# Forming the rows of each expert by TensorE products from rows on chip, in place of scatters, row loads and transposes

## What is computed

```python
def moe_swiglu(h, router, wg, wu, wd):
    probs = jax.nn.softmax((h @ router).astype(F32), axis=-1)
    vals, idx = lax.top_k(probs, TOP_K)
    vals = vals / jnp.sum(vals, axis=-1, keepdims=True)
    combine = jnp.sum(jax.nn.one_hot(idx, N_EXPERTS, dtype=F32) * vals[..., None], axis=-2)
    out = jnp.zeros(h.shape, F32)
    for e in range(N_EXPERTS):
        out = out + combine[..., e:e + 1] * swiglu(h, wg[e], wu[e], wd[e]).astype(F32)
    return out.astype(h.dtype)
```

## Time and profile before

| | |
|---|---|
| median of 3 runs | 1541.55 us (1540.8 to 1542.12) |
| profiled execution, its own time | 1543.34 us |
| its span (first to last instruction) | 1541.5 us |
| mean granted TensorE clock | 0.996 |
| TensorE busy | 1511.2 us |
| VectorE, ScalarE, GpSimd busy | 643.9, 404.6, 86.6 us |
| HBM read, written | 473.48 MB, 40.34 MB |
| first expert product | 682.63 us into the span |

### The profile page before, as it was taken

The page is one execution under the profiler, slowest core; times in us unless marked ns, Lnnn a source line. Parts: engine busy times, 40 slices in busy tenths (PEclk is TensorE's granted clock), DMA queues, the critical chain, the costliest instruction groups (busy, mean ns, idle before and its releaser), DMA issues.

```text
span 1541.5 us, 31601 instructions
## 1 busy us (share of the span) xinstructions
PE 1511.2 (98%) x14136; PEld 903.7 (59%) x14136; DVE 643.9 (42%) x1025; ACT 404.6 (26%) x613; POOL 86.6 (6%) x118
## 2 busy tenths in 40 slices
PE   9999999999999999999999999999999999999986
PEld 7888889999999999864333333333333333333322
DVE  7566878677656897551301301301311312112034
ACT  4444666544455547530000010010010000000001
POOL 1122221000000011010000000000000000000001
PEclk9999999999999999999999999999999999999998
DMA  9687786688656545569999999999999999999995
GB/s 373 223 287 268 258 291 216 201 275 280 223 179 209 199 164 196 233 234 418 426 408 427 426 425 427 424 419 429 405 424 430 395 423 427 401 427 416 423 427 249
DMA packets 136937, 515.88 MB, mean 335 GB/s; under 512 B 6488, under 2 KB 58912, under 8 KB 128480
## 3 DMA queue, kind: packets, MB, share of 16 engines
q1 hardware_dynamic: 116672, 450.03, 73.7%
q0 software_dynamic: 15968, 57.97, 10.2%
q10 hardware_dynamic: 4160, 5.84, 1.1%
HBM read 473.48 MB, written 40.34 MB: 333 GB/s over the span
## 4 chain that ended last, share of the span: by engine, by line
issue 53%; PE 37%; DVE 3%; ACT 1%; DMA 1%; POOL 0%; POOLq 0%; ACTq 0%; DVEq 0%
PE ps L2020 35%; DMA ring<-y_scr,expert_arena 1%; PE ps L2233 1%; DVE ring L1458 0%; POOL y_scr L962 0%; ACT ring_low_parts L1019 0%; DVE expert_arena L1969 0%; PE ps L2360 0%; DVE expert_arena L1986 0%; DVE ring_low_parts L1408 0%; DVE expert_arena L1976 0%; DVE expert_arena L1894 0%; ACT arena L1196 0%; PE ps L2481 0%; DVE arena L1748 0%
## 5 line engine op out<-in xcount | busy, mean ns | idle before, releaser
L2020 PE MATMUL ps<-ring,expert_x_turned 128*32 128x448 f32 x5152 | 488.8, 539 | 1.6 <-issue 0.8
L2020 PEld LDWEIGHTS ps<-ring,expert_x_turned 128*32 128x32 f32 x5152 | 169.5, 110 | 318.1 <-issue 316.2
L2020 PE MATMUL ps<-normed_high,ring_low_parts 128*128 128x264 f32 x1344 | 267.2, 290 | 0.4 <-DVE normed_low L1392 0.4
L2020 PE MATMUL ps<-ring,expert_hidden_turned 128*32 128x512 f32 x2360 | 257.4, 595 | 6.0 <-DMA ring<-in_moe_w_down 6.0
L1408 DVE TENSOR_TENSOR ring_low_parts<-ring,ring_low_parts 128x1024 fp32r<-128x1024 f32 (+3 forms) x184 | 209.1, 1142 | 84.6 <-ACT ring_low_parts L1019 84.2
L1019 ACT CAST ring_low_parts<-ring 128x1024 fp32r<-128x1024 f32 (+3 forms) x184 | 180.8, 983 | 222.9 <-PE ps L2020 214.3
L1947 DVE TENSOR_TENSOR expert_arena<-expert_arena,ps 128x1344 f32<-128x1344 f32 (+1 forms) x16 | 23.9, 1496 | 481.8 <-PE ps L2020 481.8
L2020 PEld LDWEIGHTS ps<-normed_high,ring_low_parts 128*128 128x128 f32 x1344 | 214.9, 189 | 5.4 <-issue 4.2
L2020 PEld LDWEIGHTS ps<-ring,expert_hidden_turned 128*32 128x32 f32 x2360 | 76.8, 110 | 184.0 <-issue 174.4
L2020 PE MATMUL ps<-normed_low,ring_low_parts 128*128 128x264 f32 x640 | 159.3, 284 | 0.0
L2020 PE MATMUL ps<-h_parts,ring_low_parts 128*128 128x264 f32 x1056 | 129.6, 285 | 0.0
(11 more groups left out here) (294 smaller groups left out, 1157.0 us busy)
## 6 DMA issues: line engine op xcount, KB each, us to landing
ring<-in_moe_w_gate SPq DMA_DIRECT2D x64, 1792.0 KB, 12.0
ring<-in_moe_w_down SPq DMA_DIRECT2D x47, 2048.0 KB, 13.6
ring<-in_moe_w_up SPq DMA_DIRECT2D x48, 1792.0 KB, 12.2
expert_piece_slot<-in_moe_w_up SPq DMA_DIRECT2D x16, 1792.0 KB, 13.0
ring<-in_ret_w_in SPq DMA_DIRECT2D x8, 2048.0 KB, 11.1
ring<-in_state_retention POOLq DMA_DIRECT2D x32, 512.0 KB, 6.6
out_ret_s<-ring POOLq DMA_DIRECT2D x32, 512.0 KB, 4.0
ring<-in_hg_w_in SPq DMA_DIRECT2D x8, 2048.0 KB, 8.0
```

What stands on the lines that cost most here:

```text
L2020: return nc.tensor.matmul(out, lhsT, rhs, start=first, stop=last)
```

## The change

For every visit the rows are now formed turned, by TensorE from x_tok: `gather_x` takes x_tok itself (every eighth column, 128 of them) as weights and the selection gsel (token by place) as the moving side, so that the sum in PSUM is already xe but for the gain; VectorE multiplies with the gain (`take_expert_x`). That is 8 k x 3 token tiles = 24 products of 128 columns of weights by 96 (64) columns. In the loop they stand behind piece 17 (GATHER_BEHIND) and write banks 6 and 7; VectorE makes the selection of the next visit behind the first hidden transpose. h_tok, the scatters, the row loads, the transposes of xe and the gain rows by partition are gone; the ranks for all experts are kept and swapped by visit (`by_visit`). TensorE also forms rows behind the last visit (for a further round, which here does not come). FEW keeps the places as they are: only visit 7 has 64. The core of the diff:

```diff
-C_LAST = 64
-GROUPS = [TG] * (NE - 1) + [C_LAST // 32]
+C_FEW = 64
+FEW = (7, )
+GROUPS = [C_FEW // 32 if v in FEW else TG for v in range(NE)]
...
-        X_AT, X_AT_LAST = 12, 2
+        GATHER_BEHIND = 17
...
-            def load_rows(i):
-                sp.dma_start(x_row, y_scr[bass.ds(i * C, P), :]).then_inc(x_row_in, 16)
-
             for t in range(EP):
-                if t == X_AT:
-                    sp.wait_ge(x_scattered, 96)
-                    load_rows(2)
...
-                    if t == (X_AT if v < NE - 1 else X_AT_LAST):
-                        sp.wait_ge(xe_ok, i + 1)
-                        load_rows(i + 2)
...
-            freed(pool, ("lv", 4, 3))
-            pool.dma_start(g_row, ins["norm_ffn_g"][1].partition_broadcast(P)).then_inc(rows_in, 16)
-            filled(pool, ("hvar", 0))
-            for c in range(4):
-                pool.dma_start(g_group[32 * c:32 * c + 32, 0, :],
-                               ins["norm_ffn_g"][1][256 * c:256 * c + 256].partition_broadcast(32)).then_inc(rows_in, 16)
-            filled(pool, ("ho", 3))
-            nc.gpsimd.memset(x_tok[:, 2, :], 0.0).then_inc(x_pad_ok, 1)
-            pool.wait_ge(h_tok_ok, 3)
+            pool.dma_start(moe_gain, ins["norm_ffn_g"][1].rearrange("(p k) -> p k", k=KD)).then_inc(rows_in, 16)
             pool.wait_ge(rows_ok, 1)
-            pool.wait_ge(xe_ok, 1)
-            for t in range(3):
-                m = P if t < 2 else NS
-                for w in range(2):
-                    pool.indirect_dma_start(y_scr[:, :], bass.IndirectOffsetOnAxis(ap=rowi[0:m, w, t:t + 1], axis=0),
-                                            h_tok[0:m, t, :], None).then_inc(x_scattered, 16)
...
-            link(V.scalar_tensor_tensor(out=reff, in0=rk[:, 0:3, 0], scalar=1.0, in1=mm_[:, :, 0], op0=ALU.add, op1=ALU.mult))
-            for t in range(3):
-                m = P if t < 2 else NS
-                i = V.tensor_scalar(gsel[0:m, t, :], cc("slot")[0:m], reff[0:m, t:t + 1], rstd_tok[0:m, t:t + 1],
-                                    ALU.is_equal, ALU.mult)
-            i.then_inc(sel_ok, 1)
-            V.tensor_tensor(r1, rk[:, 0:3, :].unsqueeze(1).to_broadcast([P, 2, 3, 8]), oab, ALU.mult)
+            link(V.scalar_tensor_tensor(out=rank_at, in0=rk[:, 0:3, :], scalar=1.0, in1=mm_, op0=ALU.add, op1=ALU.mult))
...
+            def selection(v, numbers):
+
+                for t in range(3):
+                    m = P if t < 2 else NS
+                    i = V.tensor_scalar(gsel[0:m, t, 0:32 * GROUPS[v]], numbers[0:m, 0:32 * GROUPS[v]],
+                                        rank_at[0:m, t, v:v + 1], rstd_tok[0:m, t:t + 1], ALU.is_equal, ALU.mult)
+                i.then_inc(sel_ok, 1)
+
+            def rank_of_further_round(v):
+
+                V.tensor_scalar(rank_at[:, :, v], rank_at[:, :, v], -32.0 * GROUPS[v], None, ALU.add)
+
+            selection(0, cc("slot"))
...
+            link(V.max(fewest, fewest_in))
+            link(V.tensor_scalar(rounds_f[:, 4:5], fewest[:, len(FEW) - 1:len(FEW)], -float(C_FEW), 1.0, ALU.is_lt, ALU.add))
...
+                V.tensor_copy(expert_at, cc("exp8"))
+                V.tensor_copy(places, cc("slot"))
+                link(V.max_index(fewest_ix, fewest, fewest_in))
+                link(V.tensor_copy(fewest_expert, fewest_ix))
+                for n, v in enumerate(FEW):
+                    link(V.tensor_scalar(swap_at, expert_at, fewest_expert[:, n:n + 1], None, ALU.is_equal))
+                    at = swap_at.unsqueeze(1).to_broadcast([P, 10, 8])
+                    link(V.tensor_tensor(swap_tmp, by_visit, at, ALU.mult))
+                    link(V.reduce_sum(swap_of, swap_tmp, AX.X))
+                    link(V.tensor_tensor(swap_by, by_visit[:, :, v], swap_of, ALU.subtract))
+                    link(V.tensor_tensor(swap_tmp, at, swap_by.unsqueeze(2).to_broadcast([P, 10, 8]), ALU.mult))
+                    link(V.tensor_tensor(by_visit, by_visit, swap_tmp, ALU.add))
+                    link(V.tensor_copy(by_visit[:, :, v], swap_of))
+                V.tensor_copy(visit_expert, expert_at).then_inc(order_ok, 1)
...
+                V.tensor_tensor(row_g, rowf, vt, ALU.add)
+                link(V.tensor_tensor(rowi, rowf, vt, ALU.add))
+                dve.sem_inc(rows_ok, 1)
...
-            def normed_rows(t):
-
-                m = P if t < 2 else NS
-                freed(dve, ("tok", t, 1))
-                V.scalar_tensor_tensor(out=h_tok[0:m, t, :], in0=x_tok[0:m, t, :], scalar=rstd_tok[0:m, t:t + 1],
-                                       in1=g_row[0:m, :], op0=ALU.mult, op1=ALU.mult).then_inc(h_tok_ok, 1)
...
+            def take_expert_x(v, q, o):
+
+                w = 32 * GROUPS[v]
+                return V.tensor_tensor(xe[:, 4 * q:4 * q + 4, 0:w], o[:, 0:4 * w].rearrange("p (k s) -> p k s", k=4),
+                                       moe_gain[:, 4 * q:4 * q + 4].unsqueeze(2).to_broadcast([P, 4, w]), ALU.mult)
+
+            dve.wait_ge(rows_in, 32)
+            for q in range(2):
+                filled(dve, ("first", q))
+                i = take_expert_x(0, q, bank(("first", q)))
+                frees(i, ("first", q))
+            freed(dve, ("first", 1))
+            dve.sem_inc(xe_ok, 1)
...
-                t0, t1 = 2 * q, min(2 * q + 2, TG)
-                filled(dve, ("first", q))
-                frees(V.tensor_tensor(first_rows[:, t0:t1], bank(("first", q))[:, 0:256 * (t1 - t0)].rearrange("p (t n) -> p t n", n=256),
-                                      g_group.to_broadcast([P, t1 - t0, 256]), ALU.mult), ("first", q))
-                freed(dve, ("first", q))
-                i = turn_rows(first_rows, t0, t1)
-            i.then_inc(xe_ok, 1)
...
-                    dve.wait_ge(x_row_in, i * 16 + 16)
-                    for t in range(GROUPS[(e + 1) % NE]):
-                        for c in range(4):
-                            j = V.transpose(xe[32 * c:32 * c + 32, :, 32 * t:32 * t + 32],
-                                            x_row[32 * t:32 * t + 32, 256 * c:256 * c + 256].rearrange("p (f b) -> p b f", b=KD))
-                    j.then_inc(xe_ok, 1)
+                        if h == 0:
+                            selection((e + 1) % NE, places)
+                            dve.wait_ge(sel_ok, i + 2)
+                            rank_of_further_round((e + 1) % NE)
...
+                    for q in range(2):
+                        dve.wait_ge(x_full, i * 2 + (q + 1))
+                        j = take_expert_x((e + 1) % NE, q, ps[:, 6 + q, :])
+                    j.then_inc(xe_ok, 1)
...
-            for t in range(TG):
-                q = t // 2
-                if t % 2 == 0:
-                    claim(("first", q))
-                for s in range(3):
-                    freed(pe, ("tok", s, 1))
-                    for c in range(4):
-                        j = mm(bank(("first", q))[32 * c:32 * c + 32, 256 * (t % 2):256 * (t % 2) + 256],
-                               gsel[:, s, 32 * t:32 * t + 32], x_tok[:, s, 256 * c:256 * c + 256], s == 0, s == 2)
-                if t in (1, 2):
-                    close(j, ("first", q))
+            def gather_x(q, o, w):
+
+                for k in range(4 * q, 4 * q + 4):
+                    for s in range(3):
+                        m = P if s < 2 else NS
+                        i = mm(o[:, w * (k % 4):w * (k % 4) + w],
+                               x_tok[0:m, s, :].rearrange("t (p k) -> t k p", k=KD)[:, k, :], gsel[0:m, s, 0:w],
+                               s == 0, s == 2)
+                return i
+
+            for s in range(3):
+                freed(pe, ("tok", s, 1))
+            for q in range(2):
+                claim(("first", q))
+                close(gather_x(q, bank(("first", q)), C), ("first", q))
             freed(pe, ("rk", 0))
             pe.sem_inc(w_used, 1)
-            keep_busy(("hw", 5), 512, 384)
+            keep_busy(("hw", 5), 128)
...
+                        if t == GATHER_BEHIND:
+                            if e == 0:
+                                pe.wait_ge(last_sel_ok, r * TL + (1 + TL))
+                            pe.wait_ge(sel_ok, n + 2)
+                            for q in range(2):
+                                gather_x(q, ps[:, 6 + q, :], 32 * GROUPS[(e + 1) % NE]).then_inc(x_full, 1)
...
+            mm(ps[0:32, last_bank[2], 0:1], ident[:, 0:32], ident[:, 0:1])
+            pe.wait_ge(xe_ok, last + 2)
```

More of the change, by code:

```diff
@@ L491, in hybrid_step @@
         marks = part(earena, RB + 418, 32)
-        last_sel = part(sel_mem, 0, TG, NT)
+        last_sel = part(sel_mem, 0, TL, NT)
         pos_wide = part(earena, 8512, 3, P)
@@ L501, in hybrid_step @@
         ixf = part(earena, RB + 160, 3, 8)
-        oab = part(earena, RB + 184, 2, 3, 8)
+        by_visit = part(tables, 0, 10, 8)
+        expert_at, rank_at = by_visit[:, 0], by_visit[:, 1:4]
+        oab = part(tables, 32, 2, 3, 8)
+        swap_tmp = part(tables, 80, 10, 8)
```

(39 more changed lines are left out.)

52 lines of the change are left out of this document (18 added, 34 removed).

## The result

The changed kernel takes 1685.93 us (median of 4 runs, 1684.88 to 1686.38) against 1541.17 (4 runs, 1539.97 to 1542.12) for the one before: a ratio of 1.0939, interval 1.092 to 1.0958. The forecast was 1595.0 us in a range of 1574 to 1647. The direction was right; the loss of 145 us is almost three times the 53.5 forecast, and lies outside the range. The profiled execution has a span of 1683.8 us at a mean clock of 0.956.

What follows compares the result with a forecast made beforehand. TensorE was taken to bind visits 0 to 6, late weights adding 11.1 us to the last. With g = 7.8 us a gather, 9g - 16.7 gave + 53.5 on 1541.55: 1595.0 us, range 1574 to 1647.

Steps and rivals of the forecast that it cites:

- What bounds the kernel: Expert stage: TensorE has no idle time in visits 0 to 6 (108.21 us each); DMA costs the last visit 11.1 us.
- I take the unit-stride value, since that ratio is VectorE's, and may be the transpose's own price: Gather's weight loads of every eighth float: priced as unit stride, 7.8 us a visit, not doubled to 13.3.
- rival 1: Gather: strided weight loads at half rate, 0.115 us more a record, g 13.3 us, + 103.0, 1644.6 us; chance 0.27.
- g: TensorE's added time for one visit's gather of 48 records: 8 x 0.955 + 0.15 = 7.8 us.
- No clock below 1.0 before it ends: Changed profile's last visit: TensorE's clock not below 1.0 before its end, the 1.2 GHz stretch moving behind it.
- So g - 11.1: Last visit: TensorE needs 72.15 + g against 83.2 us before, because weights are no longer late.
- So g - 4.8: Before the visits: gather's start to first expert product goes from 6.0 us to g + 1.2.
- The tail, - 0.8: After the last visit: end rows gathered before TensorE is done, VectorE's low parts no longer held by early sums; - 0.8 us.
- Everything costed at nothing: VectorE's selections and gain products, TensorE's new waits, SP and POOL: covered or off the path, nothing added.
- The sum: Whole kernel: 7g, g - 11.1, g - 4.8 and - 0.8 make 9g - 16.7, + 53.5 us at g 7.8.
- Rival 2: Gather: no price for changing the row count, g 5.7 us, + 34.6, 1576 us; chance 0.10.
- Rivals 3 and 4: Gather hidden, DMA sets the end, 1525 to 1530 us (0.03); or partly hidden, g near 1.9, 1541.5 us (0.02).

Runs made afterwards that it cites:

- e4: Changed kernel without the gather in the visits; two products of 384 columns carry its signals, the gather ahead of visit 0 stays: 1563.68 us, 1.0131.
- h7: Changed kernel with rows formed untransposed: selection as 32-column weights, x_tok moving by 256 columns, all token tiles at 128 rows: 1567.57 us, 1.0158.
- i1: e1 with all three token tiles at 128 rows, gather in one stretch behind piece 17: 1582.25 us, 1.0266.
- g5: e1 with the gather spread one k at a time behind eight pieces, in visit 0 too: 1612.01 us, 1.0448.
- e3: Changed kernel with one k of the gather behind each of pieces 10 to 17 in visits 1 to 7, visit 0 as it was: 1664.69 us, 1.0783.
- e2: Changed kernel with the third token tile padded to 128 rows, strided weights kept: 1647.89 us, 1.0679.
- h6: g5 with the third token tile padded to 128 rows: 1596.79 us, 1.0362.
- e1: Changed kernel with gather weights read at unit stride, gate and up weights loaded in matching row order: 1636.26 us, 1.0598.

## Why the prediction was wrong, and where it was right

**What bounds the kernel**: right. TensorE has no slack in visits 0 to 6; in every run the excess over 108.21 us is what was put on TensorE (e4's two products 1.6; the gathers of h7 3.9, i1 5.7, g5 9.1, e3 15.2 us).

**The failed step, "I take the unit-stride value, since that ratio is VectorE's, and may be the transpose's own price".** It isn't VectorE's alone: weights at every eighth float start every 0.24 us (e2), at unit stride every 0.115 (i1). The terms around it held. The 0.955 us for one k with 128 and 8 rows, plus 0.15 for entering, makes 1.105; g5 has 9.12 / 8 = 1.14. And rival 1's price of 0.115 us for each record was right in size: e3 to g5 gives 0.13. I had both prices and chose between them by the wrong argument, and the 7.8 us for g are 6.4 us too low (14.25 at full clock), before the clock is counted. The one I gave against rival 1, that TensorE streams columns twice as fast as it loads weights, so that half a rate wouldn't hold a load up, fell to e2: e2's records differ from i1's in the stride of the weight loads alone, and they start every 0.24 us, not every 0.115. It had also taken its columns from the mixer's products (0.45 ns each); in the fp32 records of this stage a column takes 0.84 ns (448 in 0.376 us), hardly less than the 0.9 ns of a load's element.

The rule of the Trainium skill (Advanced Engine Details and Errata, section SBUF Cachelines), that each new line costs, was the one that held, and it has no number; the runs here put it at 2.1 times for an fp32 load of 128 columns. They compare neighbours with a step of 32 bytes alone; that the line's 16 bytes are the limit is not shown, for no step in between was tried. The same skill (TensorE: Matmul & The Clock Gate, section LDWEIGHTS) gives a load's time by its columns alone, whatever the rows; for 128 columns its formula makes an estimate of 107 ns. i1's 112 to 115 ns between starts agree; e2's 240 don't, for the stride, and the 0.16 us for each change of the row count (g5 to h6) isn't in it either.

**The missing term: the clock.** A strided gather with measured sizes and the clock full is 14.1 + 0.15 = 14.25 us; the changed kernel's gather lasts 15.08, and some 2.4 us more lie in the down blocks behind it. So about 3.2 us a visit, some 26 us over the whole span (an estimate, worked out below), come from TensorE falling to 1.2 GHz in a long stretch of short products between weight loads. "No clock below 1.0 before it ends" was wrong: it fell in every gather. I had met such a fall in the earlier trace rows, behind a wait, and looked for it there only; here TensorE waits for nothing that the profile calls a wait, is busy for all the 3.16 us ahead of the fall, and the clock falls all the same. e3 shows that the long stretch brings it: the same records in eighths, clock full. With unit stride alone (e1) or 128 rows alone (e2) the fall shrank, with both it went (i1).

**"So g - 11.1"**, the last visit: wrong by 4.9 us in the changed kernel (94.6 - 72.15 - 17.5) and by 7.6 in e4 (- 1.9 for - 9.5). The premise that "the DMA has its whole ring of eight filled when visit 7 begins" failed, by about two and a half pieces, since slots come free as TensorE uses them: pieces 15 and 17, which I had landing about 40 and 50 us into the visit (37.4 and 47.4 by the terms given), landed 47.1 and 56.8 us in. Of the 11.1 us only what lay behind the gather's place came back. With the gather spread the whole 11.1 us did come back (e3's 87.5 us are 72.15 + 15.2, g5's 81.6 us near 72.15 + 9.1), so in one stretch it stands too late for this term. Beside 9g it is small.

**"So g - 4.8"**, the start: right. With the 14.9 us that the gather takes there it gives + 10.1; measured + 9.8. (By this term the first expert product was due at 685.6, not "near 685.4"; it came at 692.52.) **The tail, - 0.8**: right in this kernel (14.2 us against 15.0). In e4, g5 and h6, whose last visits take 81 to 82 us, it takes 16.6 to 17.6 us, and TensorE waits 2.6 to 3.7 us there for VectorE's low parts, so the term doesn't hold for every size of g. **Everything costed at nothing** (VectorE's selections and gain products, the new waits, SP and POOL): right. In e4 no wait of TensorE appears in the visits, and VectorE is busy 13.6 us of a visit instead of 19.

**The sum** with measured g: 7 x 17.4 + 11.4 + 9.8 - 0.8 = 142.2 us of a span that grew by 142.3. By rival 1 it was 103.0; by the measured size of a strided gather without the clock it would have been 9 x 14.25 - 16.7 + 4.9 = 116.5; the difference to 142.2, 25.7 us, is put down to the clock. **Rival 2** (5.7 us) was wrong as a forecast, because the row count does cost, and the stride; with unit stride and the rows padded it is what happens: i1's excess is 5.67. **Rivals 3 and 4** asked for g under 1.9 us, and the cheapest form found needs 3.9.

## What to carry to other kernels

When an operand is read in a new direction, price the read by a row with that stride or take the strided price as the likeliest: a rule and a neighbour's ratio that point the same way outweigh an argument why this engine should be spared. An engine that is the bound pays for every instruction given to it; moving work onto it from a queue that it doesn't wait for can pay only where its own work is cut at the same time. The version with three short visits cuts it, though how much the move itself has to do with that gain isn't shown. Before counting on filled buffers, ask when their slots come free, and not how much time the DMA has had.

## What the runs showed of the hardware that I had not expected

- The granted clock can fall with no wait in the trace: 128x96 products whose strided weight loads start every 0.24 us or more lost it 3.2 us into the gather, for 17.07 us, the last 5.15 under the dense work behind it. At 1.2 GHz the strided loads still start every 0.24 us, while unit-stride loads go from 0.112 to 0.214 us, so TensorE's clock doesn't set the pace of the strided ones.
- Which gathers lose the clock isn't just a matter of length: 14.1 us in eighths don't, 9.0 to 15.1 us in one stretch do, 5.53 us in one stretch don't. Nothing between 5.5 and 9.0 us was tried.
- Zero rows added are faster than a change of shape: 8 products (16 records) of 8 rows made into 128 rows save 1.3 us a visit where they are spread, with the clock full, and 0.33 us a k in one stretch (e1 against i1).
- With the operands exchanged, so that the weights are 32 columns on each of four column groups and x moves, a gather of the same rows takes 3.88 us instead of 5.53 (h7, i1), though it issues 72 records instead of 48.
